# Retention square sums as two f32r products behind the next unit's last projection piece, with a slab released one tile earlier and a first-convolution piece moved ahead of small sums

## The chip, the cores and the metric

The kernel runs on one core of a Trainium2 chip. The metric is the device time of one execution in microseconds (us); the time before is 2447.64 us, the median of three runs. The five engines named below are TensorE (PE; its weight loads are listed as PEld), VectorE (DVE), ScalarE (ACT), GpSimd (POOL) and SyncE (SP), which only issues DMAs. Each has its own instruction queue and they meet at semaphores.

## What is computed

A trunk of two layers on x (1024 tokens by 1024 channels), in float32. Each layer has a mixer and a SwiGLU block, with an RMS norm ahead of each whose scale and shift come from a conditioning vector c (`silu(c) @ ada_w + ada_b`). Layer 0's mixer is a gated convolution beside a four-head retention; layer 1's is stick-breaking attention with eight heads. The change touches mostly the norm inside retention:

```python
r = retention(q, k, v)
r = rms_norm(r, ret_norm_g.reshape(RET_HEADS, RET_HEAD_DIM))   # mean of squares over the 128 of a head
r = jax.nn.silu(g) * r.reshape(bsz, s_len, RET_DIM)
return jnp.concatenate([a_out, r], axis=-1) @ w_out
```

## The kernel before

**Products.** Activations are held transposed, channels on the partitions, tokens along the free axis in two halves of H = 512. A float32 product is made of three f32r products: each operand is split into a high part (rounded to f32r) and a low part (the rest), and `three` issues high x high, low x high and high x low (L911, L916, L917). Weights come in slabs of 128 x 1024 (512 KB) by DMA from SP; POOL splits each slab into a ring of slots (L883 the high, L887 the low part, in four quarters each). A slab's load waits until the slab two before it has been split.

**Retention phase (`ret`).** There are eight units: unit u is head u // 2 and token half h = u % 2. A unit has four projections (kinds: 0 is v, 1 is q, 2 is k, 3 is the gate), each in two pieces of 12 matmuls (`ret_piece`). While PE works on unit u's scores and weights, it is fed with the pieces 0 to 5 (v, q, k) of unit u+1 (`ret_fill`), for the last unit with pieces of the output projection. The order on PE in a unit is: gate pieces, score tiles 0 and 1, piece 0, weight tile times v (`pv`) 0, ..., `v_turn(u+1)`, pv 3, piece 4, square sum (`ret_stat`), piece 5, conditioning sums (`ada_group`).

The four weight tiles of a unit are made on DVE: score tile times decay (L2406), high part (L2099), low part `r_wp` (L2101). When pv 3 is done, ACT copies the result from psO to `r_osb` and squares it into `r_osq`; both count the semaphore `r_ocp`. `ret_stat` multiplies `r_osq` by a matrix of 1/128 in plain float32 (L1126), which gives the mean over the head's 128 channels on all partitions, in the PSUM bank psM. ACT makes 1/sqrt of it with Ln and Exp, into `r_r`, and DVE's `finish(u)` (L2417, L2420) scales `r_osb` by it, during the next unit.

psM serves many small results in turn: `misc` lets PE write it only when the reader of the one before has counted `misc_read`. The order is written in `RET_MISC`: for each unit ..., the square sum ("stat"), then the conditioning sums ("ada"). So L962, which sums `ada_acc` over the partitions, waits for ACT's Ln of the square sum and for DVE's last product of `ada(4u+3)` (L2113).

DVE's order at the end of unit u: `v_low(u+1)`, `rotate(u+1, 0)` (q), at even u `q_decayed` (L2372), `ada(4u+3)`, `qk_low(u+1, 0)` (L2367), at even u `q_decayed_low` (L2377), the conditioning columns (L2121), then of unit u+1: `rotate` of k (L2355 to L2360), at even units `k_dec` from a freshly loaded decay row (L2440), `qk_low`, `finish(u)`, `ada`, weight tile 0. ACT's order there: the copy and the Square, high part of q, Ln, Exp, then at even u the high part of the decayed query `r_qd`, at odd u the issue of the next head's decay loads (L1645, L1646). `r_w32` holds a weight tile before its split, at the place in SBUF that the change uses again.

**First convolution (`first_conv`).** The first projection runs channel tile by channel tile (`k_major(h, slabs, ks)`). `first_direct` multiplies the last block of conditioning weights with c by 32 matmuls of one column (L997). `first_cols` sums others over the partitions by matmuls of one column (L988); DVE's scale and shift for tiles 4 to 7 depend on both.

**Output projection of layer 1 (`out1`).** Eight slabs; slab 4 goes where attention's temporaries lay, slab 5 to `w_split3`, where attention's q and k lay. POOL holds slab 4 until `s_wst` says that DVE has split the last of the 12 weight tiles of the last head. The residual `xT` is reloaded from DRAM by ACT at the same count, in two DMAs of 2048 KB, since it shares its place with attention's tiles. DVE adds the projection's result to it (L2486), which frees the PSUM bank.

Of the kernel before, what the change touches and what calls it, by code (L numbers as in the profile page):

```python
# [21 lines left out]
F32 = mybir.dt.float32  # L22
# [8 lines left out]
H = 512  # L31
# [136 lines left out]
def build(nc, a):  # L168
# [4 lines left out]
    with ExitStack() as ctx:  # L173
# [87 lines left out]
        r_w32 = at("r_w32", XO + 24 * KB, [H])  # L261
        r_osb = at("r_osb", XO + 26 * KB, [H])
        r_osq = at("r_osq", XO + 28 * KB, [H])
        r_r = at("r_r", XO + 30 * KB, [H])
        r_wp = at("r_wp", WO + 32 * KB, [RPAR, 2, H], F32R)
        r_o32 = at("r_o32", WO + 44 * KB, [H])
# [109 lines left out]
        r_wst = sem("r_wst")  # L376
        r_pv = sem("r_pv")
        r_ocp = sem("r_ocp")
        r_rs = sem("r_rs")
        r_on = sem("r_on")  # L380
        r_ohi = sem("r_ohi")
# [71 lines left out]
        def M(phase, i, k):  # L453
            return C.at("misc", phase, i, k)[1] + 1
# [367 lines left out]
        def _(pool):  # L822
# [20 lines left out]
            for phase, iters, P_ in STREAM:  # L843
                def body(i):
                    for s in range(P_):
# [25 lines left out]
                        if phase == "out1" and s == 4:  # L871
                            pool.wait_ge(s_qk3, 12 * SB_HEADS)
                        if phase == "out1" and s == 4:
                            pool.wait_ge(s_wst, 3 + 2 * NT * SB_HEADS)

                        if phase == "out1" and s == 3:
# [26 lines left out]
        def _(pe):  # L903
# [107 lines left out]
            def first_conv():  # L1011
# [23 lines left out]
                x_turn(6)  # L1035
                k_major(0, (1,), (2, 3))
                x_turn(7)
                pe.wait_ge(misc_read, M("norm0", 0, 1) - 1)
                first_direct()
                k_major(0, (2,), range(4))  # L1040
                first_cols(1, 0)
                first_cols(1, 1)
                x_root_pe(1)
# [78 lines left out]

            def ret_stat(u):

                pe.wait_ge(r_ocp, 2 * u + 2)
                misc("ret", 0, RET_MISC.index(("stat", u)), [lambda: nc.tensor.matmul(  # L1126
                    psM[:], ones_head, r_osq[:], start=True, stop=True)])

            def out_piece(phase, h, m, part=None, only=None):

# [20 lines left out]
            def ret_phase(u):  # L1151

                ret_piece(u, 3, 0)
                ret_piece(u, 3, 1)
                scores(u, 0)
                scores(u, 1)
                if u % 2 == 0:
                    k_turn(u)
                ret_fill(u, 0)
                if u % 2:  # L1160
                    inter(u)
                pv(u, 0)
                scores(u, 2)
                ret_fill(u, 1)
                pv(u, 1)
                scores(u, 3)
                ret_fill(u, 2)
                if u % 2 == 0:
                    state(u)
                pv(u, 2)  # L1170
                ret_fill(u, 3)
                if u + 1 < UNITS:
                    v_turn(u + 1)
                pv(u, 3)
                ret_fill(u, 4)
                ret_stat(u)
                ret_fill(u, 5)
                ada_group("ret", 0)(u, RET_MISC.index(("ada", u)))

            ret_piece(0, 0, 0)  # L1180
# [314 lines left out]
        def _(act):  # L1495
# [211 lines left out]
            def ret_phase(u):  # L1707
# [28 lines left out]
                fn(r_osb[:], psO[:], ACT.Copy).then_inc(r_ocp, 1)  # L1736
                act.wait_ge(r_ocp, 2 * u + 1)
                fn(r_osq[:], r_osb[:], ACT.Square).then_inc(r_ocp, 1)
                if u + 1 < UNITS:
                    qk_high(u + 1, 0)  # L1740
                act.wait_ge(misc_done, RM("stat", u))
                fn(r_r[:], psM[:], ACT.Ln, bias=EPS).then_inc(misc_read, 1)
                act.wait_ge(misc_read, RM("stat", u))
                fn(r_r[:], r_r[:], ACT.Exp, scale=-0.5).then_inc(r_rs, 1)
                if h == 0:
# [342 lines left out]
        def _(dve):  # L2088
# [333 lines left out]
            def out_low(u):  # L2422
# [8 lines left out]
                    hi, lo = hT[0][:, h, KT - 1], hT[1][:, h, KT - 1]  # L2431
                V.tensor_tensor(lo, r_o32[:], hi.bitcast(F32), ALU.subtract).then_inc(r_olo, 1)

            def ret_phase(u):

                i, h = divmod(u, NH)
# [22 lines left out]
                if u + 1 < UNITS:  # L2459
                    v_low(u + 1)  # L2460
                    rotate(u + 1, 0)
                    if h == 0:
                        q_decayed(u + 1)
                ada("ret", 0, 4 * u + 3)
                if u + 1 < UNITS:
                    qk_low(u + 1, 0)
# [284 lines left out]
            ada("ret", 0, 4 * u + 2)  # L2751
            weight(u, 3)
            ada("ret", 0, 4 * u + 3)
            out_step("out0", 0)
            out_step("out0", 1)
            finish(u)
# [165 lines left out]
```

## Time and profile before

| | |
|---|---|
| median of three runs | 2447.64 us (2446.96 to 2449.67) |
| profiled execution: its own time, and its span | 2449.88 us, 2448.1 us |
| PE busy | 2408.2 us, 98% |
| DVE, ACT, POOL busy | 65%, 34%, 24% |
| chain that ended last, by engine | PE 91%, DVE 3%, DMA 2%, issue 2% |
| square sums in retention | 8, each of two passes, from 227.2 to 437.5 us |
| granted TensorE clock, mean over the span | 0.996 of full |

Times in the rows are microseconds from the span's start. A matmul's busy time overlaps that of the next one, so the distance from one start to the next is what counts; f32r matmuls of 512 columns have 0.39 of busy time each. A bracket such as `[0.66 <-DVE r_wp L2101]` is the idle time of the engine ahead of the instruction and what ended it.

### The profile page before, as it was taken

Reading aid. Unit: us, or ns where it says so; the run is one execution under the profiler, and the core shown is the slowest. Engines: PE = TensorE matmul, PEld = TensorE weight load, DVE = VectorE, ACT = ScalarE, POOL = GpSimd, SP = SyncE. Lnnn points to the kernel's source line nnn. Section 1 sums busy time; section 2 is a strip of 40 time slices with the busy share of each in tenths; the row PEclk is TensorE's granted clock in tenths of the full one; section 3 lists DMA queues with packets and bytes.
Section 4 is the critical chain, followed back from the end, with each engine's and each line's share of the span. In section 5 each row is a group of like instructions: output and inputs, shape, how many; then the busy total and the mean of one; then the engine's idle time right before and its main releaser. Section 6 shows DMA issues by size and latency. Waiting matters only on the chain.

```text
span 2448.1 us, 31399 instructions
## 1 busy us (share of the span) xinstructions
PE 2408.2 (98%) x10938; PEld 1987.2 (81%) x10938; DVE 1583.0 (65%) x2543; ACT 830.4 (34%) x1489; POOL 595.5 (24%) x964
## 2 busy tenths in 40 slices
PE   6999999999999999999999999998999999999999
PEld 5888888888888888888778888887888888888887
DVE  6636777388667665765777777776587666665222
ACT  4102333144333340000466666664253333320001
POOL 4344333300000004455143333334100000015340
PEclk9999999999999999999999999999999999999999
DMA  8543446623342349666211111116323333456331
GB/s 284 173 138 99 134 133 205 204 78 112 104 129 95 112 129 351 225 228 210 78 53 44 44 43 44 43 54 222 121 74 108 121 104 111 129 202 229 147 121 69
DMA packets 268606, 324.40 MB, mean 133 GB/s; under 512 B 8458, under 2 KB 168356, under 8 KB 268324
## 3 DMA queue, kind: packets, MB, share of 16 engines
q1 hardware_dynamic: 239552, 257.45, 31.9%
q10 hardware_dynamic: 28900, 65.04, 7.5%
q8 instruction: 79, 1.29, 0.2%
q14 instruction: 75, 0.61, 0.1%
HBM read 240.67 MB, written 81.79 MB: 132 GB/s over the span
## 4 chain that ended last, share of the span: by engine, by line
PE 91%; DVE 3%; DMA 2%; issue 2%; POOL 1%; ACT 1%; SPq 0%; DVEq 0%; ACTq 0%; POOLq 0%
PE psG L911 24%; PE psG L917 23%; PE psG L916 23%; PE psZ L917 4%; PE psZ L916 4%; PE psZ L911 4%; PE psM L1347 1%; PE psO L911 1%; PE psG L1388 1%; PE psO L916 1%; PE psO L917 1%; PE psZ L1377 1%; DMA ada_raw<-in_ada_w 1%; DMA w_raw<-in_ev_w_in 1%; PE psM L962 1%
## 5 line engine op out<-in xcount | busy, mean ns | idle before, releaser
L883 POOL TENSOR_SCALAR w_split<-w_raw 128x256 fp32r<-128x256 f32 x448 | 199.4, 471 | 1773.3 <-DMA w_raw<-in_ffn_w_down 1091.6
L911 PE MATMUL psG<-h_hi,w_split 128*128 128x512 f32 x1080 | 436.1, 404 | 7.2 <-DVE h_lo L2168 3.8
L916 PE MATMUL psG<-h_lo,w_split 128*128 128x512 f32 x1080 | 425.4, 394 | 0.0
L917 PE MATMUL psG<-h_hi,w_split 128*128 128x512 f32 x1080 | 425.3, 394 | 0.0
L887 POOL TENSOR_TENSOR w_split<-w_raw,w_split 128x256 fp32r<-128x256 f32 x448 | 359.2, 832 | 0.0
L2714 DVE SCALAR_TENSOR_TENSOR xT<-psG,mod,xT 128x512 f32<-128x512 f32 x192 | 143.0, 749 | 212.3 <-PE psG L917 211.9
L911 PE MATMUL psG<-hid,w_split 128*128 128x512 f32 x704 | 276.3, 393 | 0.0
L911 PE MATMUL psG<-h_hi,f_w 128*128 128x512 f32 x704 | 275.2, 391 | 0.6 <-PE psG L917 0.6
L917 PE MATMUL psG<-hid,w_split 128*128 128x512 f32 x704 | 274.5, 390 | 0.0
L916 PE MATMUL psG<-hid,w_split 128*128 128x512 f32 x704 | 274.3, 390 | 0.0
L916 PE MATMUL psG<-h_lo,f_w 128*128 128x512 f32 x704 | 274.3, 390 | 0.0
L917 PE MATMUL psG<-h_hi,f_w 128*128 128x512 f32 x704 | 274.2, 390 | 0.0
L1514 ACT ACTIVATE f_w<-f_raw 128x512 fp32r<-128x512 f32 x256 | 158.8, 629 | 314.6 <-PE psG L917 148.0
L911 PEld LDWEIGHTS psG<-h_hi,w_split 128*128 128x128 f32 x1080 | 205.6, 190 | 53.6 <-issue 5.5
L917 PEld LDWEIGHTS psG<-h_hi,w_split 128*128 128x128 f32 x1080 | 204.8, 190 | 44.6
L916 PEld LDWEIGHTS psG<-h_lo,w_split 128*128 128x128 f32 x1080 | 205.5, 190 | 42.8 <-issue 3.4
L2495 DVE TENSOR_TENSOR f_w<-f_raw,f_w 128x512 fp32r<-128x512 f32 x256 | 174.5, 688 | 101.0 <-ACT f_w L1514 100.4
L911 PEld LDWEIGHTS psG<-h_hi,f_w 128*128 128x128 f32 x704 | 132.2, 188 | 29.1 <-issue 1.9
L917 PEld LDWEIGHTS psG<-hid,w_split 128*128 128x128 f32 x704 | 132.2, 188 | 27.9
L916 PEld LDWEIGHTS psG<-h_lo,f_w 128*128 128x128 f32 x704 | 132.2, 188 | 27.8 <-issue 0.5
L917 PEld LDWEIGHTS psG<-h_hi,f_w 128*128 128x128 f32 x704 | 132.2, 188 | 27.3
L916 PEld LDWEIGHTS psG<-hid,w_split 128*128 128x128 f32 x704 | 132.3, 188 | 27.1 <-issue 0.2
(300 smaller groups left out, 4027.7 us busy)
## 6 DMA issues: line engine op xcount, KB each, us to landing
hid<-f_spill SPq DMA_DIRECT2D x44, 1024.0 KB, 9.4
f_spill<-f_stg SPq DMA_DIRECT2D x80, 512.0 KB, 2.7
f_raw<-in_ffn_w_gate SPq DMA_DIRECT2D x44, 512.0 KB, 3.9
f_raw<-in_ffn_w_up SPq DMA_DIRECT2D x44, 512.0 KB, 4.6
w_raw<-in_ffn_w_down SPq DMA_DIRECT2D x44, 512.0 KB, 6.1
ada_raw<-in_ada_w SPq DMA_DIRECT2D x40, 512.0 KB, 4.1
ada_raw<-in_ada_w ACTq DMA_DIRECT2D x40, 512.0 KB, 4.5
w_raw<-in_ev_w_in SPq DMA_DIRECT2D x28, 512.0 KB, 4.0
```

Of the source, the lines that this page charges most:

```text
L883: nc.gpsimd.tensor_scalar(slot[:, 0, part], raw[:, part], 1.0, 1.0, ALU.mult, ALU.mult).then_inc(hi_done, 1)
L887: lo = nc.gpsimd.tensor_tensor(slot[:, 1, part], raw[:, part], slot[:, 0, part].bitcast(F32), ALU.subtract)
L911: mm = nc.tensor.matmul(o, st[0], mv[0], start=first, stop=False, **kw)
L916: nc.tensor.matmul(o, st[0], mv[1], start=False, stop=False, **kw)
L917: return nc.tensor.matmul(o, st[1], mv[0], start=False, stop=end, **kw)
L962: misc(phase, i, mk, [lambda k=k: nc.tensor.matmul(psM[:, k:k + 1], ada_acc[:, k], consts[:, 5, 0:1], start=True, stop=True) for k in rang ...
L1347: misc(phase, i, 2 * off + e, [lambda: nc.tensor.matmul(psM[:], ones_head, sq[:], start=True, stop=True)])
L1377: mm = nc.tensor.matmul(zbank[t % ZRING][:, c0:], split_c[:, 1], s_s[:, t % SRING, n, c0:], start=False, stop=n == 1, skip_group_check=True)
L1388: mm = nc.tensor.matmul(s_run[:, c0:], split_c[:, 2], s_s[:, t % SRING, n, c0:], start=j == 4 * h + 3 and n == 0, stop=n == 1, skip_group_ ...
L1514: return nc.scalar.activation(o, i_, f, **kw)
L2495: V.tensor_tensor(slot[:, 1], src, slot[:, 0].bitcast(F32), ALU.subtract).then_inc(fw_ready, 1)
L2714: V.scalar_tensor_tensor(x, psG[:, b], mod[:, g2:g2 + 1], x_old[:, 1 - h, m] if j == 0 else x, ALU.mult, ALU.add).then_inc(bank_read[b], 1)
```

## The change

Three edits. (1) The square sum of a retention unit: ACT squares `r_osb` a second time, with the output rounded to f32r (`r_osqh`, at the place of `r_w32`), DVE takes the low part (`square_low`, in the place of `r_osq`), and PE multiplies both by a matrix of -1 in f32r; Ln gets the scale -1/128. It is issued behind piece 5 in place of piece 4. (2) In the first convolution the piece of slab 2 over tiles 0 to 3 goes ahead of `first_direct`. (3) POOL's slab 4 of `out1` waits for one weight tile less, slab 5 for all.

```diff
+        r_osql = at("r_osql", XO + 28 * KB, [H], F32R)
+        r_osqh = at("r_osqh", XO + 24 * KB, [H], F32R)
...
                         if phase == "out1" and s == 4:
+                            pool.wait_ge(s_wst, 3 + 2 * (NT * SB_HEADS - 1))
+                        if phase == "out1" and s == 5:
                             pool.wait_ge(s_wst, 3 + 2 * NT * SB_HEADS)
...
                 x_turn(7)
+                k_major(0, (2,), range(4))
                 pe.wait_ge(misc_read, M("norm0", 0, 1) - 1)
                 first_direct()
-                k_major(0, (2,), range(4))
...
             def ret_stat(u):
-                pe.wait_ge(r_ocp, 2 * u + 2)
-                misc("ret", 0, RET_MISC.index(("stat", u)), [lambda: nc.tensor.matmul(
-                    psM[:], ones_head, r_osq[:], start=True, stop=True)])
+                pe.wait_ge(r_osql_in, u + 1)
+                misc("ret", 0, RET_MISC.index(("stat", u)), [
+                    lambda: nc.tensor.matmul(psM[:], split_c[:, 2], r_osqh[:], start=True, stop=False),
+                    lambda: nc.tensor.matmul(psM[:], split_c[:, 2], r_osql[:], start=False, stop=True)])
...
                 ret_fill(u, 4)
+                ret_fill(u, 5)
                 ret_stat(u)
-                ret_fill(u, 5)
                 ada_group("ret", 0)(u, RET_MISC.index(("ada", u)))
...
                 fn(r_osq[:], r_osb[:], ACT.Square).then_inc(r_ocp, 1)
+                fn(r_osqh[:], r_osb[:], ACT.Square).then_inc(r_osqh_in, 1)
...
-                fn(r_r[:], psM[:], ACT.Ln, bias=EPS).then_inc(misc_read, 1)
+                fn(r_r[:], psM[:], ACT.Ln, scale=-1.0 / HEAD, bias=EPS).then_inc(misc_read, 1)
...
+            def square_low(u):
+                dve.wait_ge(r_osqh_in, u + 1)
+                V.tensor_tensor(r_osql[:], r_osq[:], r_osqh[:].bitcast(F32), ALU.subtract).then_inc(r_osql_in, 1)
...
                     if h == 0:
                         q_decayed(u + 1)
+                square_low(u)
                 ada("ret", 0, 4 * u + 3)
...
             ada("ret", 0, 4 * u + 3)
+            square_low(u)
             out_step("out0", 0)
```

## Rows read from the trace of the kernel before

**Rows 1.** The page, busy time of PE (share of the span).
```profile
PE 2408.2 (98%) x10938; PEld 1987.2 (81%) x10938; DVE 1583.0 (65%) x2543; ACT 830.4 (34%) x1489; POOL 595.5 (24%) x964
```
**Rows 2.** Waits, 170 to 470 us: us in total, times, longest.
```profile
PE psO L911 <- DVE r_wp L2101: 2.6, 4, 0.7
PE psM L962 <- DVE ada_acc L2113: 1.4, 4, 0.3
DVE k_dec L2440 <- DMA q_dec<-in_decay: 0.7, 2, 0.5
```
**Rows 3.** Timeline of PE, unit 0 to 1: start, duration, instruction, idle before.
```profile
227.18 1.02 PE L1126 MATMUL psM<-r_osq,consts 128*128 128x512 f32 x2
...
231.31 1.05 PE L962 MATMUL psM<-consts,ada_acc 128*128 128x1 f32 x8 [0.35 <-DVE ada_acc L2113]
...
243.24 0.50 PE L911 MATMUL psO<-r_wp,r_v 128*128 128x512 f32 x1 [0.66 <-DVE r_wp L2101]
```
**Rows 4.** The chain of waits, 250 to 330 us: start, share of the chain, instruction.
```profile
257.59 0.86 PE psM L1126 x2
258.45 0.23 PE psG L911
```
**Rows 5.** Timeline of DVE, unit 0 to 1.
```profile
229.73 1.53 DVE L2113 SCALAR_TENSOR_TENSOR ada_acc<-ada_raw,c_act,ada_acc 128x512 f32<-128x512 f32 x2
231.17 0.68 DVE L2367 TENSOR_TENSOR r_q<-r_t,r_q 128x512 fp32r<-128x512 f32 x1
231.77 0.69 DVE L2377 TENSOR_TENSOR r_qd<-r_u,r_qd 128x512 fp32r<-128x512 f32 x1
...
236.34 1.16 DVE L2367 TENSOR_TENSOR r_k<-r_t,r_k 128x512 fp32r<-128x512 f32 x1 [0.70 <-ACT r_k L1514]
```
**Rows 6.** Timeline of ACT, unit 0 to 1.
```profile
225.42 0.63 ACT L1514 ACTIVATE r_osq<-r_osb 128x512 f32<-128x512 f32 x1
...
229.23 0.58 ACT L1514 ACTIVATE r_r<-psM 128x512 f32<-128x512 f32 x1
...
230.38 0.61 ACT L1514 ACTIVATE r_qd<-r_u 128x512 fp32r<-128x512 f32 x1
```
**Rows 7.** Timeline of PE, unit 1 to 2.
```profile
261.06 0.95 PE L962 MATMUL psM<-consts,ada_acc 128*128 128x1 f32 x8
...
271.84 0.39 PE L911 MATMUL psO<-r_wp,r_v 128*128 128x512 f32 x1
```
**Rows 8.** Timeline of ACT's queue and of DVE, unit 1 to 2.
```profile
259.89 0.34 ACTq L1645 DMA_DIRECT2D decay<-in_decay  x1
...
265.58 0.17 DVE L2440 TENSOR_SCALAR k_dec<-decay 128x4 f32<-128x4 f32 x1 [0.53 <-DMA q_dec<-in_decay]
...
270.11 0.69 DVE L2101 TENSOR_TENSOR r_wp<-r_w,r_wp 128x512 fp32r<-128x512 f32 x1
```
**Rows 9.** Timeline of PE, first convolution.
```profile
43.66 4.30 PE L997 MATMUL psM<-c_act,ada_first 128*128 128x1 f32 x32 [1.37 <-DMA ada_first<-in_ada_w]
47.82 0.78 PE L911 MATMUL psG<-h_hi,w_split 128*128 128x512 f32 x1
...
53.08 2.00 PE L988 MATMUL psM<-consts,ada_acc 128*128 128x1 f32 x16
...
58.17 0.80 PE L911 MATMUL psG<-h_hi,w_split 128*128 128x512 f32 x1 [2.09 <-DVE h_lo L2168]
```
**Rows 10.** Timeline of POOL, low part of slab 2.
```profile
40.11 4.30 POOL L887 TENSOR_TENSOR w_split<-w_raw,w_split 128x256 fp32r<-128x256 f32 x4
```
**Rows 11.** Stretches of time: us, PE busy (instructions), granted clock, DMA share, GB/s.
```profile
46.60:47.80 1.20, 1.20 (x7) 0.50 1.01 291
```
**Rows 12.** Timeline of DVE, last weight tile but one of layer 1.
```profile
1687.34 0.69 DVE L2101 TENSOR_TENSOR s_w<-s_w,s_w 128x512 fp32r<-128x512 f32 x1
```
**Rows 13.** Waits of PE, 1150 to 2448 us.
```profile
PE psG L911 <- DVE xT L2486: 3.1, 1, 3.1
```
**Rows 14.** The chain of waits, 1684 to 1760 us.
```profile
1692.37 9.25 DMA xT<-x_spill
```

More of the change, by code:

```diff
@@ L378, in build @@
         r_ocp = sem("r_ocp")
+        r_osqh_in = sem("r_osqh_in")
+        r_osql_in = sem("r_osql_in")
         r_rs = sem("r_rs")
```

## The prediction

> **What bounds the kernel now.** I read the page's busy times first, then the waits of TensorE (PE) over the retention phase, then the timelines of PE, VectorE (DVE) and ScalarE (ACT) around one square sum of either kind, and last the two places outside retention. The page shows PE busy for 98% of the span [rows 1], so work on another engine counts only where PE waits for it. In the 270 us of the retention phase PE waits eight times, 4.0 us in all [rows 2]: at each even unit once for the conditioning sums (L962) and, some 12 us later, once for `r_wp`, the first decayed score tile of the next unit. At odd units PE never stands still. So DVE already leads at even units, with nothing to spare, and an instruction put into its queue there is paid in full.
>
> **Retention: the gain.** One square sum holds PE for 0.86 us [rows 4]. Two f32r products of the same size should go at the pace of the projection's, which the chain of waits has at 0.23 us each [rows 4], 0.46 the pair: 0.40 us less, eight times 3.2 us. This is the whole gain.
>
> **Retention: even units** (u = 0, 2, 4, 6; times of unit 0). The order becomes piece 5, square sum, conditioning sums. Piece 5 now begins at 227.18, where the sum stood [rows 3], and takes 12 x 0.23 = 2.7, so to 229.9. The sum needs `square_low`, which DVE reaches behind `q_decayed`, at 229.73 [rows 5]. Its ACT input, one more Square of 0.63 behind the one at 225.42 [rows 6], is there by 226.7, hidden in ACT's idle time ahead of r_q and Ln. For the DVE operation itself the nearest rows are the low parts at 231.17 and 231.77, which take 0.68 and follow one another at 0.60 [rows 5]; the same form at 236.34, while GpSimd (POOL) splits a slab, takes 1.16. I take 0.60 on DVE's queue (bounds 0.6 and 1.1), done at 230.4. PE waits from 229.9 to 230.5, and its pair ends, with the drain of the last, near 231.2.
>
> Now comes what the move uncovers. The conditioning sums write the same bank psM, so PE may not begin them before ACT's Ln has read the square sum. Before, piece 5 covered that. Now Ln runs 231.2 to 231.8 (0.58 [rows 6]), and DVE's last conditioning product, pushed by `square_low` from 231.26 to 231.86, ends at the same time. L962 begins at 231.9 against 231.31: PE +0.6.
>
> The larger effect runs through ACT. Behind Ln come Exp and the high part of the decayed query; in the trace r_qd starts 1.15 behind Ln (229.23 to 230.38 [rows 6]) and takes 0.61. With Ln at 231.2 it ends near 233.0. DVE wants its low part (L2377) at 231.77 [rows 5]; it now starts at 233.0, +1.3. Queued behind it on DVE are the conditioning columns, the rotation of k, its low part, `finish`, two conditioning products and the first weight tile, for which PE waits already (243.24, 0.66 idle [rows 3]). That chain is without slack, so PE's start there moves by the whole 1.3, which contains the 0.6. Four times 1.3 is 5.2 us.
>
> **Retention: odd units** (times of unit 1). DVE has no `q_decayed`, so `square_low` is done before PE ends piece 5 at 257.43+2.73 = 260.16. The pair and its drain end at 260.8, Ln at 261.4. L962 starts at 261.44 against 261.06 [rows 7]: PE +0.4, the saving of 0.4 included. DVE was waiting for L962 and shifts alike. Besides, ACT issues the next head's decay loads behind Exp, at 259.89 [rows 8]; Ln is 1.6 late, so these loads too. `k_dec` waits for them at 265.58 and goes to 267.1. The first weight tile, 270.80 before, is then ready at 272.4, PE wants it at 271.84+0.4 = 272.2: 0.2 more. In units 3 and 5 the wait for the load is 0.2 and nothing [rows 2], and the 1.0 us of slack between 270.80 and 271.84 holds. Unit 7 has no next unit; its `finish` is 2.4 late, but what needs it comes tens of us later. Sum: 0.6 + 3 x 0.4 = 1.8. Retention together +7.0 us, bounds 4.0 (PE's own shifts alone, 4 x 0.6 + 4 x 0.4) and 9.0 (each `square_low` at 1.1).
>
> **The first convolution.** Slab 2's low part ends at 40.11+4.30 = 44.41 [rows 10], so the piece of slab 2 can't begin when the direct sums did, at 43.66 [rows 9]; PE stands 0.75 longer. In return its 12 products run in front of the 32 one-column matmuls. Before, the granted clock fell to 0.50 (1.2 GHz) near 46.6 [rows 11], some 3 us into these, and the 12 products behind took 47.82 to 53.08, 5.3 us. In front, at 2.4 GHz, they take 2.7, to 47.2. The small ones then take 4.2 to 51.3, and the 16 column sums (1.9 before, on mostly the high clock) 1.9 or, at the low clock, 3.7: their end is 53.2 or 55.0, against 54.95. If the clock falls again some 3 us into the small ones, near 50, it is the second. I take 0 in three cases of four and -1.8 in one: -0.4. Bounds: -4.4 (also the 5.3 us behind 58.17 [rows 9] at the high clock) and +4 (the clock falls in the longer wait and all of it runs at half pace).
> The Trainium skill (TensorE: Matmul & The Clock Gate, "What's actually happening") says that the default is the throttled state and that activity releases it; by that, denser work ahead of the small matmuls could keep the high clock through them.
>
> **The output projection of layer 1.** POOL's split of slab 4 waits until DVE has split the last weight tile, at 1692.35, just ahead of the issue in [rows 14]; with one tile less it waits for 1687.34+0.69 = 1688.0 [rows 12], 4.3 us less. Nothing on PE waits for that slab: PE's wait there, 3.1 us, is for `xT` [rows 13], whose reload is issued at 1692.37, when the last tile is split, and takes 9.25 [rows 14]. So there is no gain, and two ways to lose. First, POOL's work now meets DVE's last tile (multiply, high, low) of 1.8 us; its two operations with both inputs in SBUF go from 0.69 to about 1.16 if they suffer as the one in [rows 5]: about +1.0 on the issue of the reload. Second, slab 6's load, freed by slab 4, is issued 4.3 us earlier, together with the reload: 512 KB beside 2048 KB that take 9.25, so 0 to 2.3 more; I take 0.7. Sum +1.7, bounds 0 and +3.3.
> The Trainium skill (SBUF — State Buffer, on the shared port pair) calls it an exclusive lock: the second to come blocks fully. By that a POOL subtraction, a quarter of the 4.30 of [rows 10], could hold each of the two DVE operations for up to 1.1, +2.2 in place of +1.0. It speaks against this edit.
>
> **Sum.** +7.0 - 0.4 + 1.7 = +8.3. The profiled execution has a span of 2448.1 and a time of 2449.88, 2.2 above the median of 2447.64; a difference made of its rows I add to the median: 2455.9. What a measurement can tell from no change is 0.2%, 4.9 us.
>
> **Rivals.**
> (a) Only PE's own shifts show. If DVE's chain has slack that the rows hide (its collisions with POOL, 1.16 against 0.68, may fall away when it runs 0.7 later against POOL), retention costs 4.0, the rest about 0: 2451.6. For it: the chain has slowed operations, as the one of 1.16 at 236.34. Against it: POOL's slabs are released by PE's progress, which moves along by 0.6, so the collisions move too. 0.13.
> (b) The clock stays high in the first convolution, -4.4 in place of -0.4: 2451.9. For it: dense work first. Against it: the longer wait ahead, and over 5 us of small matmuls in one piece behind. 0.10.
> (c) The reload loses more, +3.3, and the retention chain's `square_low` meets POOL, +9.0: 2459.6. Against it: the operation behind the place of `square_low`, at 229.73, runs at its usual length. 0.12.
> (d) Other side: the release of psM costs nothing, because Ln's read is seen by PE while it drains, and DVE's low part isn't late. Then only 0.4 a unit is left, 3.2, with -1.8 from the convolution: 2442.6. It decides if L962 starts less than 0.05 behind the square sum's end; but the Ln row alone has 0.58. 0.04.
> The forecast itself, 2452.7 to 2458.5: 0.61.
>
> **Range and chances.** From (a) below to (c) above: 2450.8 to 2459.3; outside are (d) and the edges of (a) and (c), about 0.15. Slower by over 0.2% is above 2452.5: the forecast, (c) and a little of (b): 0.76. Within 0.2%: (a) and most of (b): 0.20. Faster: (d), 0.04.
>
> **What would show it.** In the profile after: an idle time of PE ahead of the square sum at even units (0.5 us, for `r_osql`); one ahead of L962 at every unit (even 0.7, odd 0.65), put down to ACT's r_r or DVE's ada_acc; L2377 with a wait for ACT's r_qd; PE's waits for `r_wp` from 2.6 us in all to 4 or more; the time from one square sum of an even unit to the next even one's, 60.0 us now, to 61.7. At 1700, PE's wait for `xT` of 4 to 5 us. In the first convolution, 12 products at the 0.23 pace and small ones behind. The prediction falls if PE's idle time in retention grows by less than 5 us, or if the start of the dense stretch (58.17) comes by more than 2 us earlier.

## The result and the profile after

The change makes the kernel slower: 2456.97 us (median of 6 runs, 2455.73 to 2460.94) against 2447.44 us for the kernel before beside it (6 runs, 2446.26 to 2450.02), a ratio of 1.0041 with an interval of [1.003, 1.0052]. Forecast were 2455.9 us, slower, and a range of 2450.8 to 2459.3. The profiled execution took 2456.85 us with a span of 2455.0; that of before had a span of 2448.1, so the two traces differ by 6.9 us, the medians by 9.5. The trace of before is that of an execution 2.4 us above its median, and four of the six traces without the edit of the first convolution begin its dense stretch 1.6 earlier than this one (below). So the differences between these two traces add up to too little.

The waits of TensorE (PE), 170 to 490 us, us in total, times, longest:

```profile
PE psM L968 <- ACT r_r L1521: 3.1, 4, 0.8
PE psM L968 <- DVE ada_acc L2121: 3.1, 4, 0.8
PE psM L1133 <- DVE r_osql L2445: 1.7, 4, 0.4
PE psG L917 <- POOL w_split L893: 1.1, 1, 1.1
PE psO L917 <- DVE r_wp L2109: 0.6, 1, 0.6
PE psZ L917 <- DVE r_k L2375: 0.4, 1, 0.4
```

They answer to [rows 2]: 4.0 us of waits have become 10.0, of which the 1.1 for POOL's `w_split` lie behind the phase. In retention that leaves 8.9, 4.9 more than before. L968 (before: L962) now waits at all eight units. But the waits for `r_wp`, which were forecast to grow from 2.6 to 4 and more, fell to 0.6. PE's timeline around the sums of unit 0 shows why one can't read the waits alone:

```profile
222.06 0.38 PE L1080 MATMUL psM<-consts,r_vsb 128*128 128x128 f32 x2
...
228.86 0.50 PE L1133 MATMUL psM<-r_osqh,split_c 128*128 128x512 f32 x1 [0.41 <-DVE r_osql L2445]
229.20 0.40 PE L1134 MATMUL psM<-r_osql,split_c 128*128 128x512 f32 x1
230.38 1.02 PE L968 MATMUL psM<-consts,ada_acc 128*128 128x1 f32 x8 [0.78 <-DVE ada_acc L2121]
...
233.25 0.63 PE L917 MATMUL psG<-h_hi,w_split 128*128 128x512 f32 x1
...
243.08 0.39 PE L917 MATMUL psO<-r_wp,r_v 128*128 128x512 f32 x1
```

Behind the two waits the projection's matmuls have 0.63 of busy time instead of 0.39: the granted clock is at its lower level, 1.2 GHz, for 3.4 us. A view by stretches (us, PE busy, granted clock, DMA share, GB/s) has it too:

```profile
228.00:232.00 4.00, 2.81 (x15) 1.00 0.60 145
232.00:236.00 4.00, 4.00 (x12) 0.57 0.35 123
236.00:240.00 4.00, 4.00 (x20) 1.00 0.45 131
```

This happens behind units 0, 2 and 4 of this execution and nowhere in retention before. In those units PE, slowed, comes to the first weight tile (243.08) after DVE has finished it (at 242.38), and has no wait for it. Behind unit 6 the clock stays up, and the forecast wait is there:

```profile
428.65 0.50 PE L917 MATMUL psO<-r_wp,r_v 128*128 128x512 f32 x1 [0.55 <-DVE r_wp L2109]
```

The VectorE (DVE) and ScalarE (ACT) rows at unit 0 show the chain that was forecast:

```profile
228.13 0.68 DVE L2445 TENSOR_TENSOR r_osql<-r_osq,r_osqh 128x512 fp32r<-128x512 f32 x1
...
231.44 0.69 DVE L2385 TENSOR_TENSOR r_qd<-r_u,r_qd 128x512 fp32r<-128x512 f32 x1 [0.59 <-ACT r_qd L1521]
```
```profile
229.63 0.60 ACT L1521 ACTIVATE r_r<-psM 128x512 f32<-128x512 f32 x1 [1.91 <-PE psM L1134]
...
230.80 0.61 ACT L1521 ACTIVATE r_qd<-r_u 128x512 fp32r<-128x512 f32 x1
```

**A measure that is free of what hides what.** I cut each period of two units into halves: from the transpose of the next unit's values (L1080) to that unit's first weighted product (`pv` 0). The *even half* holds the sums of an even unit (223.67 to 243.24 before, 222.06 to 243.08 after); the *odd half* those of an odd unit. All rows are starts on PE.

| us | even halves (units 0, 2, 4, 6) | odd halves (1, 3, 5) |
|---|---|---|
| before | 19.57, 19.56, 19.57, 19.56 | 17.93, 17.93, 17.94 |
| after | 21.02, 20.97, 20.97, 20.79 | 18.66, 18.50, 18.48 |

The even halves cost 1.23 to 1.45 more, 5.5 in all, the odd ones 1.8. From the start of the values' transpose of unit 0 to the last conditioning sum the phase grew from 244.62 us (196.04 to 440.66) to 252.07 (194.44 to 446.51), 7.45.

**Outside retention.** In the first convolution the order did what it says, and the dense stretch began 1.1 earlier, at 57.08 ([rows 9]: 58.17):

```profile
44.51 0.47 PE L917 MATMUL psG<-h_hi,w_split 128*128 128x512 f32 x1 [1.65 <-issue]
...
47.30 3.63 PE L1003 MATMUL psM<-c_act,ada_first 128*128 128x1 f32 x32
50.79 3.19 PE L994 MATMUL psM<-consts,ada_acc 128*128 128x1 f32 x16
...
57.08 0.80 PE L917 MATMUL psG<-h_hi,w_split 128*128 128x512 f32 x1 [1.18 <-DVE h_lo L2176]
```

At layer 1's output projection DVE's last weight tile met GpSimd (POOL), the reload (chain of waits: 9.25 before [rows 14]) took a little longer, and PE's wait for `xT` went from 3.1 to 4.2 [rows 13]. The rows are those of DVE, of POOL and of the chain of waits:

```profile
1696.02 0.69 DVE L2835 TENSOR_TENSOR s_w<-s_w,s_e 128x512 f32<-128x512 f32 x1 [2.42 <-ACT s_w L1521]
1696.75 0.85 DVE L2107 CAST s_w<-s_w 128x512 fp32r<-128x512 f32 x1
1697.63 1.11 DVE L2109 TENSOR_TENSOR s_w<-s_w,s_w 128x512 fp32r<-128x512 f32 x1
```
```profile
1693.91 1.51 POOL L889 TENSOR_SCALAR w_split<-w_raw 128x256 fp32r<-128x256 f32 x4 [16.06 <-DVE s_w L2109]
1695.38 3.96 POOL L893 TENSOR_TENSOR w_split<-w_raw,w_split 128x256 fp32r<-128x256 f32 x4
```
```profile
1698.78 9.83 DMA xT<-x_spill
```

The offset of the second trace against the first (PE starts) runs: -1.6 at the head of retention, +5.85 at its end, +7.24 at the statistics of the next norm, +5.56 just ahead of the last weight tiles of layer 1, +6.99 when PE resumes behind the reload, +6.96 near the end. The step of +1.4 between the second and third was in no term of the forecast (below). Neither was the one of -1.7 behind it, but that one isn't the change's: in the trace of before the granted clock fell at 1234.4 for 3.4 us, in the other it didn't fall there (1.2 of the 1.7), and PE's wait for `ada_acc` at 1112 was 0.3 shorter.

### The profile page after: what moved, and what is told of

It is laid out like the page before. It is cut to its first block, busy times and chain, and to the rows that moved or that the text cites. A ratio compares the mean times of both kernels' runs of the same rounds, so it can differ in the third digit from the quotient of the medians.

```text
span 2455.0 us, 31416 instructions
## 1 busy us (share of the span) xinstructions
PE 2409.0 (98%) x10938; PEld 1988.0 (81%) x10938; DVE 1591.1 (65%) x2551; ACT 835.4 (34%) x1497; POOL 596.7 (24%) x964
## 4 chain that ended last, share of the span: by engine, by line
PE 93%; DVE 3%; DMA 2%; ACT 1%; issue 1%; POOL 0%; ACTq 0%; SPq 0%; DVEq 0%; POOLq 0%
PE psG L917 24%; PE psG L923 24%; PE psG L922 24%; PE psZ L923 4%; PE psZ L922 4%; PE psZ L917 4%; PE psG L1395 1%; PE psO L917 1%; PE psM L1354 1%; PE psO L922 1%; PE psO L923 1%; PE psZ L1384 1%; DMA w_raw<-in_ev_w_out 1%; PE psM L968 1%; PE psG L1384 1%
```

## The experiments

Ten kernels, in three sessions; the kernel before ran beside each. Its median was 2447.33 in the first and 2448.5 in the other two, so only ratios are compared across them.

### The three edits apart

`e1_conv_alone`: the kernel before, with the piece of slab 2 ahead of `first_direct`.

```diff
+                k_major(0, (2,), range(4))
                 pe.wait_ge(misc_read, M("norm0", 0, 1) - 1)
                 first_direct()
-                k_major(0, (2,), range(4))
```

> The kernel before with only the piece of slab 2 ahead of the small sums of the first convolution. My account of the changed kernel: this edit gains 1.6 us on its own, already there at the first v transposes of retention (196.04 in the kernel before, 194.44 in the changed one), because the 12 products run at the high clock, so a ratio near 0.9993 and retention as before. Rival, by my forecast: nothing, since a longer low-clock stretch behind gives it back (0.4 us). Rival, the state of the clock differs from run to run, so the gain is between 0 and 3 us and not stable.

Measured: 2448.67 (11 runs), ratio 1.0006 [0.9997, 1.0015]. Its trace began the dense stretch at 56.85 and had a span of 2446.5, yet the median did not fall: one trace is no measure of this stage. Over all the traces of this study, kernels without the edit began the dense stretch at 58.17, 58.16, 56.55, 56.52, 56.54 and 56.65, kernels with it at 57.08, 56.85, 57.66, 59.25, 59.38 and 59.31. The same order of instructions gives starts up to 2.5 us apart, by where the clock falls. Without the edit it fell late in the 32 one-column matmuls or just behind them (46.2 to 48.3), for 3.4 us in four traces (56.5) and for 6.8 in two (58.2). With it, the three early traces have the clock at 1.00 through the twelve products; in the three late ones (e6, e8, e10) PE had stood 2.7 us ahead of the twelve products and not 1.5 to 1.8, and the clock fell 1.0 us into them. The edit's worth is lost in this, and if anything it is a loss.

`e2_slab_alone`: the kernel before, with POOL's slab 4 released one tile earlier.

```diff
                         if phase == "out1" and s == 4:
-                            pool.wait_ge(s_wst, 3 + 2 * NT * SB_HEADS)
+                            pool.wait_ge(s_wst, 3 + 2 * (NT * SB_HEADS - 1))
+                        if phase == "out1" and s == 5:
+                            pool.wait_ge(s_wst, 3 + 2 * NT * SB_HEADS)
```

> The kernel before with only slab 4 of the last output projection released one weight tile earlier. Theory: a loss of 1.4 us, all of it in PE's wait for xT (3.1 us before, 4.5 here), of which 1.0 is DVE's last tile stretched by POOL (issue of the reload from 1692.4 to about 1693.1) and the rest a slower reload; ratio 1.0006. Rival: the loss in the changed kernel came from another state of the clock there, and alone the edit costs nothing (ratio 1.0000, PE's wait 3.1).

Measured: 2450.32 (11 runs), ratio 1.0012 [1.0003, 1.0021], some 2.9 us. The trace carries 1.4 of it on the way to PE's restart: from DVE's last multiply to the restart 12.00 us before (1690.45 to 1702.45), 13.38 here. Another 1.1 lies behind it, where the clock was low for 6.8 us and not for 3.4; the same two stretches, here and then in the kernel before:

```profile
1690.00:1700.00 10.00, 7.13 (x31) 1.00 0.82 291
1700.00:1710.00 10.00, 8.67 (x26) 0.66 0.69 235
```
```profile
1690.00:1700.00 10.00, 9.31 (x42) 1.00 0.64 227
1700.00:1710.00 10.00, 7.55 (x27) 0.83 0.88 299
```

The rest of the kernel from the restart on takes 745.6 us in the trace of before and 746.8 here. This second part doesn't hang on the longer wait: it was 745.6 in the trace of the full change, whose wait was as long, and 746.8 in that of `e4_move_alone` (below), which hasn't the edit and waits 3.2. The first part does come with the edit. Over the twelve traces, DVE's last multiply to the restart takes 12.3 to 13.6 us in the six with it and 11.6 to 12.2 in the six without.

`e3_ret_alone`: the retention edit, without the other two.

> The changed kernel with the other two edits undone: only retention's square sums differ from the kernel before. Theory: retention loses 7.4 us between its first v transposes and the last conditioning sums, as in the changed kernel, and the first slab of the next stage another 1 (PE's wait for POOL), ratio 1.0033 to 1.0037. If the clock falls behind the waits only in some phases, the even units show either a stretch at 1.2 GHz and no wait for r_wp, or a wait for r_wp and no such stretch, 1.2 to 1.5 us in both cases. Rival: the loss hangs on the earlier edit (a shift of 1.6 us against the clock's phase), and alone retention loses only PE's own waits, 4.0 us, ratio 1.0016.

Measured: 2454.91 (5 runs), ratio 1.0038 [1.0024, 1.0052]. Even halves 20.78, 20.99, 21.00, 21.00, odd 18.65, 18.49, 18.48: the full change's, with the low clock now behind units 2, 4 and 6 and the wait for `r_wp` (0.54) behind unit 0. Nearly all of the loss is the retention edit's. The differences between medians are 1.3, 3.0 and 7.6 us for the three edits apart, 11.9 together against 9.5 for the full change; the intervals are too wide to tell these sums apart.

### Move or split?

`e4_move_alone`: the kernel before, with its plain sum behind piece 5. No pair, no `square_low`, no second Square.

```diff
                 ret_fill(u, 4)
+                ret_fill(u, 5)
                 ret_stat(u)
-                ret_fill(u, 5)
```

> The kernel before, its square sum still one plain float32 product, only issued behind piece 5 in place of piece 4; no square_low on DVE. Theory: the move is what costs. PE ends piece 5 at 229.9 (unit 0), the sum holds it 0.86, Ln then runs until 231.5 and the conditioning sums start 0.3 to 0.5 later than before at even units and about 0.8 later at odd ones; r_qd is late by 1.0, so the even units lose about 1.0 at r_wp. Sum 4 x 1.0 + 4 x 0.8 = 7.2 us, ratio 1.0030. Rival: the move is harmless and square_low on DVE's queue costs (0.6 at each even unit, more where POOL collides): then this is within 1 us of the kernel before.

Measured: 2455.84 (6 runs), ratio 1.0032 [1.002, 1.0044]. The move alone costs about what everything costs. PE's waits, and DVE's at unit 0:

```profile
PE psM L962 <- ACT r_r L1514: 6.2, 8, 0.8
PE psO L911 <- DVE r_wp L2101: 2.2, 4, 0.6
PE psZ L911 <- DVE r_k L2367: 1.4, 4, 0.4
PE psG L911 <- POOL w_split L887: 1.0, 1, 1.0
```
```profile
232.55 0.69 DVE L2377 TENSOR_TENSOR r_qd<-r_u,r_qd 128x512 fp32r<-128x512 f32 x1 [0.90 <-ACT r_qd L1514]
```

With plain sums and no `square_low`, L2377 still waits for ACT; the even halves are 20.50, 0.93 above before, and the odd ones 18.89 to 19.29. The clock stayed at 1.00 through retention. Against this kernel the pair saves 0.41 at odd halves (18.48 against 18.89, the 0.40 of the forecast) and loses 0.3 at the even one where the clock stays up (20.79 against 20.50): the pair waits for `square_low`, so Ln and `r_qd` come later still. The 0.5 of the other even halves lie behind a fall of the clock, which this kernel doesn't have.

### Taking the two couplings away

`e5_own_columns`: the full change, with the conditioning sums in four columns of psZ, so that they don't wait for Ln to read psM.

```diff
-                ada_group("ret", 0)(u, RET_MISC.index(("ada", u)))
+                ret_ada(u)
...
+            def ret_ada(u):
...
+                if u:
+                    pe.wait_ge(r_adr, u)
+                for k in range(4):
+                    mm = nc.tensor.matmul(psZ[:, 1, k:k + 1], ada_acc[:, k], consts[:, 5, 0:1], start=True, stop=True)
+                mm.then_inc(r_ad, 1)
```

> The changed kernel, with one thing different: the four conditioning sums of a retention unit (L968) go to four columns of psZ that nothing reads then, with semaphores of their own, so that TensorE no longer waits at them for ScalarE's Ln to have read psM. The theory (the held psM is a cost of its own): the waits of L968 for r_r, 3.1 us in 4 rows, go and nothing takes their place, the waits for ada_acc in the even units (3.1 in 4) stay, since those are for DVE's last conditioning step; about 2453.9 us against 2457.0. The rival (TensorE arrives earlier and then waits for DVE or a transfer behind it, as for r_wp, k_dec or the weight slab): the 3.1 us show up again in other rows and the time stays within 2456 to 2457.5.

Measured: 2456.18 (6 runs), ratio 1.0033 [1.002, 1.0046]. The interval overlaps that of the full change, so the median decides nothing; the trace does. The waits for `r_r` are gone, the odd halves are 17.77, 17.74 and 17.76 (18.66 to 18.48 before this edit), and the phase takes 248.72, 3.35 less than in the full change: the theory's 3.1. The even halves stay at 20.81 to 20.99.

`e6_act_order`: the full change, with ACT's high part of `r_qd` and its decay loads ahead of Ln and Exp.

```diff
                     qk_high(u + 1, 0)
-                act.wait_ge(misc_done, RM("stat", u))
-                fn(r_r[:], psM[:], ACT.Ln, scale=-1.0 / HEAD, bias=EPS).then_inc(misc_read, 1)
-                act.wait_ge(misc_read, RM("stat", u))
-                fn(r_r[:], r_r[:], ACT.Exp, scale=-0.5).then_inc(r_rs, 1)
                 if h == 0:
                     act.wait_ge(qd_mul, i + 1)
...
                     decays(i + 1)
+                act.wait_ge(misc_done, RM("stat", u))
+                fn(r_r[:], psM[:], ACT.Ln, scale=-1.0 / HEAD, bias=EPS).then_inc(misc_read, 1)
+                act.wait_ge(misc_read, RM("stat", u))
+                fn(r_r[:], r_r[:], ACT.Exp, scale=-0.5).then_inc(r_rs, 1)
```

> The changed kernel, with ScalarE's order at a unit's end different: the high part of r_qd (even units) and the issue of the next decay loads (odd units) come ahead of Ln and Exp. The prediction's theory (even units lose 0.6 us each because DVE's low part of r_qd waits for ScalarE): L2385's waits of 2.3 us in 4 go, k_dec's waits of 2.4 in 3 fall below 1, and the time falls by 2.4 to 3 us, to about 2454.3. The rival (TensorE in units 0, 2 and 4 is held by its own low clock and not by DVE, as the profile of the changed kernel shows): the two waits of DVE go as well, but TensorE's arrival moves in unit 6 alone, by 0.5 us, so that the time is 2456.2 to 2457.

Measured: 2457.66 (5 runs), ratio 1.0039 [1.0025, 1.0053]: no gain, as the rival had it. DVE's waits for ACT's `r_qd` and for the decay loads are gone. But the even halves are 20.99, 21.02, 20.23 and 22.58 (behind unit 6 the clock was low for 6.8 us): where the clock fell (units 0, 2 and 6) PE takes 21.0 or more whatever DVE does, and only where it didn't (unit 4) is DVE's earlier work seen, 20.23 against 20.79 behind unit 6 of the full change. There both kernels wait for `r_wp`:

```profile
356.27 0.68 DVE L2385 TENSOR_TENSOR r_qd<-r_u,r_qd 128x512 fp32r<-128x512 f32 x1
...
366.61 1.11 DVE L2109 TENSOR_TENSOR r_wp<-r_w,r_wp 128x512 fp32r<-128x512 f32 x1
```
```profile
367.77 0.50 PE L917 MATMUL psO<-r_wp,r_v 128*128 128x512 f32 x1 [0.65 <-DVE r_wp L2109]
```

So the late low part of `r_qd` costs 0.56 of the even half, once the clock doesn't cover it. The odd halves are 18.48 all three: the 0.2 more of unit 1 in the full change (18.66) was the late decay load.

`e8_after_late`: the full change with both of these edits, and the conditioning sums of unit u taken behind the first key piece of unit u+1.

```diff
                 ret_piece(u, 3, 0)
+                if u:
+                    ret_ada(u - 1)
                 ret_piece(u, 3, 1)
...
```

> The changed kernel with both of those and one thing more: the conditioning sums of unit u, in columns of their own, are taken behind the first projection piece of unit u+1's key (TensorE) and read behind its rotation (DVE), so that neither is waited for at the unit's end. Theory (the cluster of short waits and one-column matmuls behind the square sum is what loses the time and lowers the clock): no wait at L968, no stretch at 0.50 of the clock in the retention units, waits for r_osql of 1.7 us as before, waits for r_wp back to some 3 us in the even units, since DVE's chain is then what ends last; retention 3 us longer than in the kernel before instead of 7.5, about 2452.5 us. Rival (DVE's chain sets the end of every unit whatever TensorE does, one subtraction of 0.69 us longer per unit): TensorE's waits come back in full in front of r_wp and r_k, 0.7 us in each of 8 units and more, and the time stays above 2455.

Measured: 2453.23 (10 runs), ratio 1.0021 [1.0011, 1.0031]. The trace:

```profile
PE psZ L919 <- DVE r_k L2396: 2.3, 4, 0.6
PE psO L919 <- DVE r_wp L2124: 2.2, 4, 0.6
PE psM L1145 <- DVE r_osql L2466: 1.7, 4, 0.4
PE psG L919 <- POOL w_split L895: 1.4, 2, 1.0
```

Even halves 20.02 to 20.04, odd ones 17.48, the clock at 1.00 throughout, the phase 244.64: the time of the kernel before to 0.02, with the waits for `r_wp` back. What was forecast as a loss of 3 us is none, and 0.46 more at each even half is paid for by 0.45 less at each odd one. The 5 us that the median still shows are outside this phase. By estimate they are the slab edit's 2.9, and about 2 in the output projection of layer 0 (78.6 us from the last conditioning sum to the next norm's statistics before, 80.55 here).

`e9_before_late`: the kernel before with the same three edits and its plain sum in its old place.

> The kernel before (plain f32 square sum in its old place, ahead of the last piece) with the three edits of the run above: conditioning sums in columns of their own and taken late, ScalarE's decay work ahead of Ln. It asks whether the waits that the change lengthened were worth anything even before it. Theory: the waits for ada_acc of 1.4 us in 4 go, but DVE's chain ends no earlier, so that waits for r_wp of 2.6 grow to about 4; 2446.5 to 2447.5, no difference. Rival (TensorE's order is what sets it): 1.4 to 3 us less, 2444.5 to 2446.

Measured: 2448.65 (10 runs), ratio 1.0001 [0.9991, 1.0011]; the phase 244.61. The waits for `ada_acc` had been worth nothing, since `r_wp` came behind them: even halves 19.57 as before. Beside it the even half of `e8_after_late` shows what the pair costs DVE: `square_low` takes 0.60 of its queue, and `r_wp` comes 0.46 later.

### What lowers the clock

`e10_square_first`: the full change, with `square_low(u)` ahead of `q_decayed(u + 1)` on DVE.

> The changed kernel with DVE's low part of the square (L2445) taken ahead of the decayed query (L2380) instead of behind it, so that it is done before TensorE comes to the pair. It asks what lowers the clock in even units. If it is the two waits close together (0.41 for r_osql and 0.78 for ada_acc with one pair between them): the first goes, the second grows to about 1.2, and with one wait in one place the low stretches behind units 0, 2 and 4 go; waits for r_wp of 0.6 come back in their place, the time stays at 2456 to 2457.5. Rival (any idle TensorE of 1.2 us ahead of the one-column sums will do): the low stretches stay and so does the time. Either way even units gain nothing by TensorE's earlier pair, since DVE's conditioning step ends when it did; the period of two units stays 61.2 to 62.0.

Measured: 2457.77 (5 runs), ratio 1.0036 [1.0022, 1.0049]. The wait for `r_osql` is gone and L968 waits for 1.32 in one piece in even units; the clock fell behind units 0, 4 and 6 and not behind 2, where the even half is 20.19. Units 0 and 2, waits and the stretches of the clock:

```profile
232.12 1.05 PE L968 MATMUL psM<-consts,ada_acc 128*128 128x1 f32 x8 [1.32 <-DVE ada_acc L2121]
...
294.49 1.05 PE L968 MATMUL psM<-consts,ada_acc 128*128 128x1 f32 x8 [1.32 <-DVE ada_acc L2121]
```
```profile
234.00:238.00 4.00, 4.00 (x13) 0.65 0.34 119
294.00:298.00 4.00, 3.52 (x19) 1.00 0.73 212
```

So it isn't two waits that are needed. Over all traces with 1.1 to 1.3 us of waits just ahead of the one-column sums (full change, e3, e5, e6, e10) the clock fell behind 14 of 20 such units; behind a single wait of 0.8 or less (their odd units, every unit of e4 and e8, the kernel before) never. The same wait can be followed by a fall or not, and what decides it I can't tell from these runs.

### The pair only where it pays

`e11_odd_pairs`: the kernel before with own columns, late sums and ACT's order, and the pair in the odd units alone. First convolution and slab 4 as before.

```diff
             def ret_stat(u):
+                if u % 2 == 0:
+                    pe.wait_ge(r_ocp, 2 * u + 2)
+                    misc("ret", 0, RET_MISC.index(("stat", u)), [lambda: nc.tensor.matmul(
+                        psM[:], ones_head, r_osq[:], start=True, stop=True)])
+                    return
                 pe.wait_ge(r_osql_in, u // 2 + 1)
...
```

> The retention edit alone, kept where it should pay: the f32r pair and its low part in the odd units only, one plain f32 product in the even ones, the conditioning sums in columns of their own and late, ScalarE's decay work first; first convolution and output weights as in the kernel before. Theory (the sum of an even unit lies in the half of the period that DVE sets through r_wp, that of an odd unit in the half that TensorE sets): the even half is as before (19.6 us from the transpose of the values to the first weighted sum), the odd half 0.45 shorter, two units 59.55 instead of 60.03, some 1.8 us over the four odd units; 2446.7 beside 2448.5, a ratio of 0.9993. Rival (the odd half's gain is taken back at the next r_wp or k_dec): 60.0 and a ratio of 1.000.

Measured: 2447.55 (11 runs) beside 2448.5, ratio 0.9999 [0.999, 1.0008]. In the trace the forecast of the theory holds to 0.05: even halves 19.57 to 19.58, odd ones 17.48. An even and an odd half:

```profile
221.21 0.27 PE L1080 MATMUL psM<-consts,r_vsb 128*128 128x128 f32 x1
...
240.78 0.50 PE L917 MATMUL psO<-r_wp,r_v 128*128 128x512 f32 x1 [0.54 <-DVE r_wp L2128]
...
251.45 0.38 PE L1080 MATMUL psM<-consts,r_vsb 128*128 128x128 f32 x2
...
268.93 0.39 PE L917 MATMUL psO<-r_wp,r_v 128*128 128x512 f32 x1
```

The phase takes 242.79, 1.83 less than before. It is given back at once: from the last conditioning sum to the next norm's statistics 80.6 us pass instead of 78.6, with 1.5 of waits for POOL's `w_split` that the kernel before doesn't have. Where they come from is in the next section, under what was missing.

## Why the prediction was right, and where it wasn't

**Retention, +7.0: measured +7.45** (252.07 against 244.62). e3, which also has the layer 0 part below, is 7.6 slower by its medians and 9.3 by its ratio, with an interval of 5.9 to 12.7. The even units' 1.3 came out at 1.23 to 1.45, the odd ones' 0.4 to 0.6 at 0.55 to 0.73, the last unit's 0.4 at 0.5. The mechanism is the forecast one in part. Counted from the values' transpose, the forecast had unit 0's Ln at 7.5, `r_qd` at 8.7, L2385 at 9.3 and L968 at 8.2; they came at 7.57, 8.74, 9.38 and 8.32. Shown: the moved sum makes L968 wait (e5: without that coupling 3.35 less); the low part of `r_qd` starts 9.38 behind the transpose of the values instead of 8.10, which is the forecast 1.3; where the clock doesn't fall, the even half is set by `r_wp` (20.79), and the ACT order's part in it is 0.56 (e6, unit 4); the other 0.66 (20.23 against 19.57) goes with `square_low` (0.46 in e8).

Wrong was "PE's waits for `r_wp` from 2.6 us in all to 4 or more": they fell to 0.6. Behind three even units of four the clock fell to 1.2 GHz, PE ran late by itself, and its lateness (21.0) happens to lie 0.2 above the 20.8 that DVE's chain set at unit 6. At units 0, 2 and 4 DVE had the tile ready at 20.3 to 20.5, before PE came. The two costs lie on top of each other and don't add up, so the sum stood while its reason held in one unit of four: that the number came out is luck there. The step that failed is the one that begins with "Now comes what the move uncovers": it counted the waits of 0.41 and 0.78 ahead of the conditioning sums only as time, and didn't ask what they do to the clock.

By its own sign the prediction just falls: PE's idle time in retention was to grow by 5 us or more and grew by 4.9 (4.0 to 8.9), because the fall of the clock took the place of the waits for `r_wp`. The other signs came: 0.41 for `r_osql`, 0.78 ahead of L968 everywhere, 4.2 for `xT`, and 61.85 to 62.1 from one even unit's square sum to the next (61.7 forecast).

The forecast's 1.3 at L2377 is a lateness and not a wait, and the rows agree: DVE comes 0.7 later to it, 0.6 of it through `square_low`, and then waits 0.59 for ACT, 1.28 together.

**The gain, 0.40 a pair: right** (0.41, e4 against the full change; 0.45 at the odd halves of e8 and e11). Its worth depends on where it falls. In the even half DVE leads, and the pair's own low part costs 0.46 there (e8 against e9); in the odd half PE leads and all of it is kept.

**First convolution, -0.4: not measurable.** In the trace of the full change the twelve products took 2.8 (2.7 forecast) and the clock fell again, at 51.2 (near 50 forecast). That is behind the 32 one-column matmuls, which took 3.5 and not 4.2, so that the column sums ended 1.1 earlier than before and not at the same time. But the starts of the dense stretch differ by 2.5 us between executions, and e1's median is +1.3, with an interval of -0.7 to +3.7 by its ratio. The Trainium skill (TensorE: Matmul & The Clock Gate, "What's actually happening") has activity release the clock; here the clock stayed at 1.00 through the twelve products and the 32 one-column ones behind them (44.51 to 50.9), was 0.50 from 51.2 to 61.4, and in e6, e8 and e10 fell among the twelve products themselves.

**Output projection of layer 1, +1.7: 1.4 on the way to PE's restart, and 2.9 [0.7, 5.1] by the ratio of e2.** The collision was +0.84 on the issue of the reload (0.43 to 0.85 and 0.69 to 1.11), forecast +1.0; but the forecast had it at the multiply and the low part, and it was the cast and the low part: the multiply kept its 0.69. The reload itself took 9.83 instead of 9.25, forecast +0.7. The low clock behind the wait, 1.1 more in e2's trace and nothing in the full change's, is in no term, and the twelve traces don't show that it comes from the edit: three of the six with it have the longer stretch of 6.8, and one of the six without. DVE's two operations grew by 0.42 each, POOL's four subtractions together from 2.82 to 3.96. One by one the ends are 1697.32 (POOL), 1697.60 (DVE's cast), 1698.20 (POOL), 1698.74 (DVE's low part), 1699.34 (POOL): each lies its own undisturbed length (0.43, 0.73, 0.69, 0.74), less some 0.14, behind the end of the other engine's, as if they took turns. The Trainium skill (SBUF — State Buffer, "SBUF: two separate sides") says that the second to come blocks fully. The trace agrees with that; the +2.2 did not come because each of DVE's operations waited for the rest of one subtraction of 0.74, and not for a whole one of 1.1.

**What was missing: +1.4 in the output projection of layer 0.** PE waits there for POOL's split, 1.1 (row above), where it waited for nothing before; e3, e4, e5, e8 and e11 have 0.9 to 1.5 as well, e10 has 0.5, e6 and e9 none. The chain of waits in the trace of the full change has POOL wait for the slab's load, and the load take 7.88 instead of 5.39. ACT reloads `xT` (2048 KB) behind the last unit's `finish` and its low part, and that reload now goes out 4.0 us behind the last conditioning sum instead of 1.6, and so 2.1 us ahead of the slab load instead of 4.4. The ACT row and POOL's row behind the slab load, first before, then after, and the load in the chain of waits after:

```profile
442.29 0.37 ACTq L1705 DMA_DIRECT2D xT<-x_spill  x1
452.29 1.51 POOL L883 TENSOR_SCALAR w_split<-w_raw 128x256 fp32r<-128x256 f32 x4 [0.98 <-DMA w_raw<-in_ev_w_out]
```
```profile
450.52 0.37 ACTq L1712 DMA_DIRECT2D xT<-x_spill  x1
460.67 1.52 POOL L889 TENSOR_SCALAR w_split<-w_raw 128x256 fp32r<-128x256 f32 x4 [3.29 <-DMA w_raw<-in_ev_w_out]
```
```profile
452.58 7.88 DMA w_raw<-in_ev_w_out
```

All twelve traces agree. Where the reload goes out 1.6 to 1.9 behind the last sum (before, e1, e2, e9), the slab load takes 5.3 to 5.5 and PE doesn't wait. Where it goes out at 3.7 to 4.8, still ahead of the slab load (full change, e3, e4, e5, e8, e10, e11), the load takes 6.9 to 8.0 and PE waits. In e6 the slab load goes out first, takes 3.6, and PE doesn't wait. No run moved the reload alone. The step of the forecast that failed here is "its `finish` is 2.4 late, but what needs it comes tens of us later": the lateness of 2.4 is right, and the reload that needs it comes at once.

**Of the rivals,** (a), that only PE's own shifts count since collisions fall away, would have been 2451.6; DVE's chain did lose one collision (`finish`, 1.22 before, 0.74 after at units 0, 2 and 6) and still had the first weight tile ready 0.8 to 1.2 later. (b), a clock that stays up in the first convolution, isn't seen in any trace with the edit. (c)'s larger loss at the reload is within e2's interval. (d), a free release of psM, is refuted at the odd units by the 0.78 for `r_r`, which own columns took away (e5); at the even ones DVE's `ada_acc` holds L968 as long in any case.

## What to carry to other kernels

Moving a small sum behind a dense piece also moves every reader of its bank, and what they hold up: here the move alone cost 7.8 us of the phase, more than twice the 3.2 that the pairs were to bring. Before splitting an operation to make TensorE faster, cut the loop into stretches between two fixed instructions and see which engine sets each; the pair pays only in the half that TensorE sets. And where a new wait stands beside one-column matmuls, look at the granted clock behind it: it can hide the wait that was forecast and make a repair elsewhere (e6) look worthless. Last, follow a late result of the last unit to the transfer that it releases, and see which other transfer that will meet.

## What the runs showed of the hardware

- The granted clock fell from 1.00 to 0.50 for 3.4 us (twice 6.8) behind 14 of 20 places where PE had stood still for 1.1 to 1.3 us just ahead of eight one-column matmuls, and behind none where it had stood for 0.8 or less. In one trace a wait of 1.32 was followed by a fall at units 0, 4 and 6 and not at 2.
- Such a fall cost an even half 0.8 (21.0 against 20.2, e10), and twice, when it lasted longer, 2.4 (22.58, e6 and e10).
- A DVE cast and subtraction (128x512) and POOL's subtractions (128x256), running side by side with their tensors in SBUF, ended one behind the other: DVE's took 0.85 and 1.11 instead of 0.43 and 0.69, POOL's up to 1.24 instead of 0.74.
- A slab load of 512 KB took 5.4 us when a reload of 2048 KB had gone out 4.4 us ahead of it, and 7.9 us when it had gone out 2.1 us ahead.
